# The four context pieces ahead of the first expert product are spread over the first four expert passes

## The chip, the cores and the metric

The kernel runs on one core of a Trainium2 chip. The metric is the device time of one execution in microseconds (us); the time of a kernel is the median of its timed runs. The trace of the kernel before is one further execution, taken with the hardware profiler on. PE is TensorE (PEld its weight loads), DVE is VectorE, ACT is ScalarE, POOL is GpSimd, SP is SyncE; a name with q behind it is the sequencer of that engine.

## What is computed

Two transformer blocks over 256 tokens of width 1024, with 256 context tokens beside them. The first block ends in a mixture of 32 experts, of which each token uses two. The second block begins with a chunkwise mLSTM and a multiscale pool, run for the tokens (x) and for the context. The part of the reference that matters here:

```python
for gi in range(N_GROUPS):
    hid = (jax.nn.silu(jnp.einsum('td,edf->tef', t, w_gate[gi]))
           * jnp.einsum('td,edf->tef', t, w_up[gi])
           * combine[:, gi, :, None].astype(t.dtype))
    out = out + jnp.einsum('tef,efd->td', hid, w_down[gi])
...
ux, uc = hx @ w_in, hc @ w_in
...
hc_f, st_f = mlstm_chunkwise(qc, kc, vc, lif_c, lff_c, zero)
```

The context's side of the second block (uc, its mLSTM, its pool and its output) doesn't depend on the experts, so the kernel computes it while the experts' weights arrive.

## The kernel before

The expert stage (moe_pe, moe_act, moe_dve) runs ten passes over the 32 experts: six passes of four experts each, with 32 columns for every expert, then four passes of two experts (PASSES). Weights are read in halves of 1024 KB. One pass of four experts reads 24 of them: gate, up and down matrices, two halves each, for four experts. A pass has six half products on PE, numbered 6p to 6p+5 in the whole stage: four in project (line L2409: gate half 0, gate half 1, up half 0, up half 1) and two in down (L2426). Every half product raises the semaphore step_used when it is done.

sparse_sync on SP issues the loads of the halves in the order in which PE needs them, into a ring of nine slots (NHALF, half_slot). Load n waits on step_used until the half product that used load n-9 is done (L2282). So nine loads go out at once, and every further group of four waits for a half product of four experts. The context's weights come in halves of the same size through the queue of ACT (f_load, L1402), into four slots of their own. f_next issues the next two halves when ACT takes the last result of the tile that used the slots.

The gather of a pass (L2395) picks the tokens' rows into the pass's 128 columns; ACT copies one half of the result from PSUM to SBUF (L2456), DVE the other (take_gathered). Then come project, SiLU on ACT (L2465), the product with the up half on DVE, four transposes (L2442), ACT's copy of them (L2473), down, and the copies of its result, which ACT stores.

Between these steps each engine runs pieces of the context's work. body_pe, body_act and body_dve are generators, and one next() is one piece. fill(body, p, i) runs the pieces of position i in pass p. PE has nine positions: 0, 1 and 2 behind the first three half products, 3 behind the gather of the next pass, 4 behind the transposes, 5 and 6 behind the halves of down, 7 and 8 at the end of the pass. ACT and DVE have the same nine positions in their own order, so that piece k on one engine answers to piece k on the others. start(body) runs four pieces ahead of the first pass. In all there are 108 pieces in start and fill: 4, 16 for each of six passes, and 2 for each of four.

The context's pieces come in this order on PE: four pieces of the K projection (L1440), four of V (L1455), the gate columns (L1482, L1488), which wait for ACT's exponentials (L1629), then the heads' mLSTM steps (L1499, L1506, L1511 begin a head; L1522, L1527, L1533 follow) with the pieces of the output gate (L1471) in between, and so on to the pool (L1558) and the output projection (L1569, L1574).

Of the kernel before, what the change touches and what calls it, by code (L numbers as in the profile page):

```python
# [227 lines left out]
def build(nc, d, out):  # L228
    ctx = ExitStack()
    with ctx:  # L230
# [601 lines left out]
        def gla_pe(pe):  # L832
# [7 lines left out]
            def tiles(n):  # L840

                for _ in range(n):
                    next(fill)
# [1387 lines left out]
        PASSES = [(N_WIDE + 4 * i, 4) for i in range((NX - N_WIDE) // 4)] + [(2 * i, 2) for i in range(N_WIDE // 2)]  # L2231
# [52 lines left out]
        step_of = [n for n in range(6 * NPASS) for _ in range(PASSES[n // 6][1])]  # L2284

        FILL_FOUR, FILL_TWO = (2, 2, 2, 2, 2, 2, 2, 1, 1), (0, 0, 0, 1, 0, 1, 0, 0, 0)

        def fill(body, p, i):

            for _ in range((FILL_FOUR if PASSES[p][1] == 4 else FILL_TWO)[i]):  # L2290
                next(body, None)

        def start(body):

            for _ in range(4):
                next(body, None)

        def finish(body):
            for _ in body:
                pass  # L2300
# [19 lines left out]
        def moe_pe(pe):  # L2320
            v = pe.value_load(over[0:1, 0:1], min_val=0, max_val=1)
            at = counts()
            with pe.If(v == 0):
                sparse_pe(pe, body_pe(pe))
            after = counts()
            set_back(at)
            with pe.Else():
                dense_pe(pe)
                pe.wait_ge(acc_out, 4 * NX)
                finish(body_pe(pe))  # L2330
            assert counts() == after

        def moe_act(act, chain):
            v = act.value_load(over[0:1, 0:1], min_val=0, max_val=1)
            at, n = counts(), chain.n
            with act.If(v == 0):
                sparse_act(act, body_act(act, chain))
            after, n_after = counts(), chain.n
            set_back(at)
            chain.n = n  # L2340
            with act.Else():
                dense_act(act)
                finish(body_act(act, chain))
            assert counts() == after and chain.n == n_after
# [42 lines left out]
        def sparse_pe(pe, body):  # L2387
            def gather(p):

                pe.wait_ge(pick_ready, p + 1)  # L2390
                if p >= 2:
                    pe.wait_ge(py_out, 2 * p - 2)
                for k in range(DT):
                    for t in range(TT):
                        mm = nc.tensor.matmul(bank[2 + k // 4][:, (k % 4) * P:(k % 4 + 1) * P], hrows[:, t, k * P:(k + 1) * P], pick[:, t, :],  # L2395
                                              start=(t == 0), stop=(t == 1), skip_group_check=True)
                    if k % 4 == 3:
                        mm.then_inc(gath_mm, 1)

            def project(p, b, n, at):  # L2400

                experts = PASSES[p][1]
                w = P // experts
                for half in range(2):
                    pe.wait_ge(step_in[(n + half) % NSTEP], filled_to[n + half])
                    for k in range(4 * half, 4 * half + 4):
                        for e in range(experts):
                            rows = slice(e * w, (e + 1) * w)
                            mm = nc.tensor.matmul(bank[b][rows, :], gath[:, k, rows], half_slot[(load_at[n + half] + e) % NHALF][:, (k % 4) * 512:(k % 4 + 1) * 512],  # L2409
                                                  start=(k == 0), stop=(k == DT - 1), skip_group_check=True)  # L2410
                    mm.then_inc(step_used, 1)
                    if at + half < 3:
                        fill(body, p, at + half)

            def down(p, n):

                experts = PASSES[p][1]
                w = P // experts
                for half in range(2):
                    pe.wait_ge(step_in[(n + half) % NSTEP], filled_to[n + half])  # L2420
                    for f in range(2 * half, 2 * half + 2):
                        for side in range(2):
                            for e in range(experts):
                                rows = slice(e * w, (e + 1) * w)
                                at = (f % 2) * D + side * 512
                                mm = nc.tensor.matmul(bank[2 + side][rows, :], phid_t[:, f, rows], half_slot[(load_at[n + half] + e) % NHALF][:, at:at + 512],  # L2426
                                                      start=(f == 0), stop=(f == 3), skip_group_check=True)
                    mm.then_inc(step_used, 1)
                    fill(body, p, 5 + half)

            gather(0)
            start(body)
            for p in range(NPASS):
                pe.wait_ge(gath_out, 2 * p + 2)
                project(p, 0, 6 * p, 0)
                project(p, 1, 6 * p + 2, 2)
                if p < NPASS - 1:
                    gather(p + 1)
                fill(body, p, 3)
                pe.wait_ge(hid_out, p + 1)  # L2440
                for f in range(4):
                    mm = nc.tensor.transpose(bank[0][:, f * P:(f + 1) * P], phid[:, f * P:(f + 1) * P], ident[:])  # L2442
                mm.then_inc(phid_mm, 1)
                fill(body, p, 4)
                if p < NPASS - 1:
                    pe.wait_ge(gath_out, 2 * p + 4)
                pe.wait_ge(phid_t_out, p + 1)
                down(p, 6 * p + 4)
                fill(body, p, 7)
                fill(body, p, 8)  # L2450
            finish(body)

        def sparse_act(act, body):
            def take_gathered(p):
                act.wait_ge(gath_mm, 2 * p + 1)
                nc.scalar.copy(gath[:, 0:4, :].rearrange("p k s -> p (k s)"), bank[2][:]).then_inc(gath_out, 1)  # L2456

            take_gathered(0)
            start(body)
            for p in range(NPASS):  # L2460
                fill(body, p, 0)
                act.wait_ge(step_used, 6 * p + 2)
                if p:
                    act.wait_ge(phid_mm, p)
                nc.scalar.activation(phid, bank[0][:], ACT.Silu).then_inc(silu_out, 1)  # L2465
                fill(body, p, 1)
                fill(body, p, 2)
                if p < NPASS - 1:
                    act.wait_ge(step_used, 6 * p + 4)
                    take_gathered(p + 1)  # L2470
                fill(body, p, 3)
                act.wait_ge(phid_mm, p + 1)
                nc.scalar.copy(phid_t.rearrange("p f s -> p (f s)"), bank[0][:]).then_inc(phid_t_out, 1)  # L2473
                fill(body, p, 4)
                fill(body, p, 5)
                act.wait_ge(step_used, 6 * p + 6)
                if p:
                    act.wait_ge(rows_stored, 16 * p)
                nc.scalar.copy(py[:, 0:512], bank[2][:]).then_inc(py_out, 1)
                fill(body, p, 6)  # L2480
                act.wait_ge(py_out, 2 * p + 2)
                act.dma_start(expert_rows[p * P:(p + 1) * P, :], py).then_inc(rows_stored, 16)
                for i in (7, 8):
                    fill(body, p, i)
            finish(body)
            act.wait_ge(rows_in, 16 * 4)
            for t in range(TT):
                nc.scalar.activation(acc[:, t, :], acc[:, t, :], ACT.Copy, scale=row_w[:, 0, t:t + 1]).then_inc(rows_scaled, 1)

        def sparse_dve(dve, body, chain):  # L2490
# [10 lines left out]
            def make_pick(p):  # L2501
                o, shape, first, experts, w = slots(p, pick)
                nc.vector.tensor_tensor(o, bc(slot_no[:, 0:w].unsqueeze(1).unsqueeze(1), shape), bc(place[:, :, first:first + experts].unsqueeze(3), shape),  # L2503
                                        ALU.is_equal).then_inc(pick_ready, 1)

            make_pick(0)
            take_gathered(0)
            make_pick(1)
            start(body)
            for p in range(NPASS):  # L2510
                for i in (0, 1, 2):
                    fill(body, p, i)
# [802 lines left out]
```

## Time and profile before

| | us |
|---|---|
| median of 3 timed runs | 1648.13 |
| lowest, highest | 1647.65, 1653.49 |
| the profiled execution | 1652.92 |
| its span | 1650.8 |
| PE busy in the span | 1523.1 |
| DVE busy | 487.8 |
| ACT busy | 341.3 |

The profiled execution took 1652.92 us, of which the span from the first to the last instruction is 1650.8. The expert stage lies between about 476 and 1083 us. A busy PE is a PE that has matmuls in its pipeline, at full or at half clock. In the views of the trace a group's time runs from its first start to its last end, so groups that follow one another overlap by some tenths of a microsecond. The chain of waits counts them without that overlap.

### The profile page before, as it was taken

Reading aid. Unit: us, or ns where it says so; the run is one execution under the profiler, and the core shown is the slowest. Engines: PE = TensorE matmul, PEld = TensorE weight load, DVE = VectorE, ACT = ScalarE, POOL = GpSimd, SP = SyncE. Lnnn points to the kernel's source line nnn. Section 1 sums busy time; section 2 is a strip of 40 time slices with the busy share of each in tenths; the row PEclk is TensorE's granted clock in tenths of the full one; section 3 lists DMA queues with packets and bytes.
Section 4 is the critical chain, followed back from the end, with each engine's and each line's share of the span. In section 5 each row is a group of like instructions: output and inputs, shape, how many; then the busy total and the mean of one; then the engine's idle time right before and its main releaser. Section 6 shows DMA issues by size and latency. Waiting matters only on the chain.

```text
span 1650.8 us, 22126 instructions
## 1 busy us (share of the span) xinstructions
PE 1523.1 (92%) x9357; PEld 1057.2 (64%) x9357; DVE 487.8 (30%) x1233; ACT 341.3 (21%) x698; POOL 4.1 (0%) x8
## 2 busy tenths in 40 slices
PE   6999999999899889988989999969889999999897
PEld 3655689888774444545556655457766675888665
DVE  2200086423343321223213000047342231022571
ACT  2311151211212202022100000023211222021461
POOL 0000000000000000000000000000000000000000
PEclk9999999999799999999999999979899999999998
DMA  9989632132269999999999999932122413423100
GB/s 376 414 348 369 251 137 94 54 108 101 105 281 395 420 420 396 388 420 411 421 413 414 396 400 421 383 135 102 52 102 102 153 71 133 153 84 132 52 1 26
DMA packets 54305, 397.60 MB, mean 241 GB/s; under 512 B 6359, under 2 KB 13688, under 8 KB 16440
## 3 DMA queue, kind: packets, MB, share of 16 engines
q1 hardware_dynamic: 40384, 341.85, 51.4%
q10 hardware_dynamic: 13240, 52.16, 8.0%
q0 software_dynamic: 576, 2.10, 0.4%
q8 instruction: 77, 1.26, 0.3%
q14 instruction: 28, 0.23, 0.0%
HBM read 389.80 MB, written 6.29 MB: 240 GB/s over the span
## 4 chain that ended last, share of the span: by engine, by line
PE 81%; DMA 8%; DVE 4%; ACT 4%; issue 2%; ACTq 1%; SPq 0%; DVEq 0%; POOL 0%; POOLq 0%; PEldq 0%; PEld 0%
PE bank L692 16%; PE bank L1440 13%; PE bank L1455 8%; PE bank L2409 8%; PE bank L2426 4%; PE bank L1574 3%; PE bank L1569 3%; PE bank L526 3%; PE bank L2395 2%; PE bank L723 2%; PE bank L1146 2%; PE bank L1160 2%; DMA ring<-in_moe_w_up 2%; DMA work<-in_pool_inv 1%; PE bank L554 1%
## 5 line engine op out<-in xcount | busy, mean ns | idle before, releaser
L692 PE MATMUL bank<-H,ring 128*128 128x256 f32 (+1 forms) x960 | 245.1, 412 | 1.0 <-ACTq L297 0.7
L692 PEld LDWEIGHTS bank<-H,ring 128*128 128x128 f32 x960 | 181.3, 191 | 52.8 <-issue 28.8
L2409 PE MATMUL bank<-ring,work 128*32 128x512 f32 (+1 forms) x712 | 150.1, 646 | 9.2 <-DMA ring<-in_moe_w_up 5.2
L1440 PE MATMUL bank<-H,work 128*128 128x256 f32 x512 | 115.8, 385 | 1.1 <-issue 1.1
L1440 PE MATMUL bank<-H,ring 128*128 128x256 f32 x512 | 113.6, 381 | 0.0
L2409 PE MATMUL bank<-work 128*32 128x512 f32 (+1 forms) x312 | 109.6, 625 | 1.6 <-DMA work<-in_moe_w_up 1.6
L1440 PEld LDWEIGHTS bank<-H,work 128*128 128x128 f32 x512 | 97.2, 192 | 20.2 <-issue 7.2
L1440 PEld LDWEIGHTS bank<-H,ring 128*128 128x128 f32 x512 | 98.0, 192 | 13.7
L2409 PEld LDWEIGHTS bank<-ring,work 128*32 128x32 f32 (+1 forms) x712 | 40.2, 125 | 85.0 <-issue 72.3
L1455 PE MATMUL bank<-ring,H 128*128 128x512 f32 x192 | 83.4, 593 | 0.0
L2426 PE MATMUL bank<-ring,work 128*32 128x512 f32 (+1 forms) x312 | 69.1, 596 | 0.7 <-issue 0.7
L2426 PE MATMUL bank<-work 128*32 128x512 f32 (+1 forms) x200 | 65.3, 596 | 2.8 <-issue 1.4
L1455 PEld LDWEIGHTS bank<-ring,H 128*128 128x128 f32 x192 | 36.3, 190 | 43.8 <-issue 43.5
L1455 PE MATMUL bank<-work,H 128*128 128x512 f32 x128 | 56.9, 597 | 0.0
L526 PEld LDWEIGHTS bank<-work,csil 128*32 128x32 f32 x1536 | 42.8, 115 | 12.3 <-issue 11.0
L526 PE MATMUL bank<-work,csil 128*32 128x128 f32 x1536 | 49.9, 285 | 0.0
L2395 PEld LDWEIGHTS bank<-work 128*128 128x128 f32 x320 | 38.1, 199 | 11.2 <-issue 7.7
L1455 PEld LDWEIGHTS bank<-work,H 128*128 128x128 f32 x128 | 23.7, 190 | 31.9 <-issue 31.8
L2395 PE MATMUL bank<-work 128*128 128x128 f32 x320 | 40.0, 285 | 3.0 <-DVE work L2503 3.0
L2409 PEld LDWEIGHTS bank<-work 128*32 128x32 f32 (+1 forms) x312 | 26.8, 121 | 24.0 <-issue 22.0
L1522 PE MATMUL bank<-work 128*128 128x257 f32 x64 | 22.5, 436 | 19.7 <-DVE work L1849 16.5
L546 DVE TENSOR_TENSOR mod<-bank,vecs 128x8 f32<-128x8 f32 x24 | 4.0, 167 | 106.7 <-PE bank L537 106.7
(431 smaller groups left out, 2005.0 us busy)
## 6 DMA issues: line engine op xcount, KB each, us to landing
ring<-in_moe_w_gate SPq DMA_DIRECT2D x46, 1024.0 KB, 12.7
ring<-in_moe_w_up SPq DMA_DIRECT2D x43, 1024.0 KB, 11.4
ring<-in_moe_w_down SPq DMA_DIRECT2D x39, 1024.0 KB, 13.0
work<-in_ab_w_in ACTq DMA_DIRECT2D x28, 1024.0 KB, 9.8
ring<-in_ab_w_in SPq DMA_DIRECT2D x14, 2048.0 KB, 7.5
work<-in_moe_w_down SPq DMA_DIRECT2D x25, 1024.0 KB, 14.3
work<-in_ada_w SPq DMA_DIRECT2D x12, 2048.0 KB, 15.5
ring<-in_w_in SPq DMA_DIRECT2D x12, 2048.0 KB, 10.3
```

What stands on the lines that cost most here:

```text
L526: mm = nc.tensor.matmul(bank[5][32 * g:32 * g + 32, 0:P], csil[:, m // 12, k, :], slot_k(mod_chunk[m], k, g * P, (g + 1) * P), start=(k == ...
L692: mm = nc.tensor.matmul(tile_bank(i)[:, 0:n], weight(c, k, j * P, (j + 1) * P), rhs(k), start=(k == 0), stop=(k == kt - 1))
L723: mm = nc.tensor.matmul(bank[i % NB][:], H[:, k, t * P:(t + 1) * P], slot_k(c, k, 0, 512), start=(k == 0), stop=(k == DT - 1))
L1146: mm = nc.tensor.matmul(bank[4 + j % 2][:, half * T:(half + 1) * T], slot_w(c, k, j * P, (j + 1) * P), y[:, k, :], start=(k == 0), stop=(k ...
L1160: mm = nc.tensor.matmul(bank[6 + j % 2][:, 0:T], slot_k(c, k, (j % 4) * P, (j % 4 + 1) * P), mix[:, k, :], start=(k == 0), stop=(k == DT - 1))
L1440: mm = nc.tensor.matmul(b[:, j * T:(j + 1) * T], w_k(m, n, k, at, at + P), H[:, k, m.s], start=(k == 0), stop=(k == DT - 1), skip_group_ch ...
L1455: mm = nc.tensor.matmul(b[:], H[:, k, at:at + P], w_k(m, n, k, 0, 512), start=(k == 0), stop=(k == DT - 1))
L1569: nc.tensor.matmul(b[:, j * T:(j + 1) * T], w_q(m, OUT[r], 8 + k, j * P, (j + 1) * P), m.yp[:, k, :], start=(j + k == 0), stop=False, skip ...
L1574: mm = nc.tensor.matmul(b[:, j * T:(j + 1) * T], w_q(m, OUT[r], k, j * P, (j + 1) * P), m.ym[:, k, :], start=False, stop=(k == 7), skip_gr ...
L2395: mm = nc.tensor.matmul(bank[2 + k // 4][:, (k % 4) * P:(k % 4 + 1) * P], hrows[:, t, k * P:(k + 1) * P], pick[:, t, :], start=(t == 0), s ...
L2409: mm = nc.tensor.matmul(bank[b][rows, :], gath[:, k, rows], half_slot[(load_at[n + half] + e) % NHALF][:, (k % 4) * 512:(k % 4 + 1) * 512] ...
L2426: mm = nc.tensor.matmul(bank[2 + side][rows, :], phid_t[:, f, rows], half_slot[(load_at[n + half] + e) % NHALF][:, at:at + 512], start=(f ...
```

## The change

start is taken out, on all three engines, and with it the four pieces ahead of the first pass. FILL, a list with one row of positions for every pass, takes the place of the choice between FILL_FOUR and FILL_TWO. Its first four rows have 2 instead of 1 at position 7, so that passes 0 to 3 have 17 pieces, not 16. The sum is 108 as before. From pass 4 on, each position holds the same pieces as before.

```diff
         FILL_FOUR, FILL_TWO = (2, 2, 2, 2, 2, 2, 2, 1, 1), (0, 0, 0, 1, 0, 1, 0, 0, 0)
+        FILL = [FILL_FOUR if experts == 4 else FILL_TWO for _, experts in PASSES]
+        FILL[0] = (2, 2, 2, 2, 2, 2, 2, 2, 1)
+        FILL[1] = (2, 2, 2, 2, 2, 2, 2, 2, 1)
+        FILL[2] = (2, 2, 2, 2, 2, 2, 2, 2, 1)
+        FILL[3] = (2, 2, 2, 2, 2, 2, 2, 2, 1)
 
         def fill(body, p, i):
 
-            for _ in range((FILL_FOUR if PASSES[p][1] == 4 else FILL_TWO)[i]):
-                next(body, None)
-
-        def start(body):
-
-            for _ in range(4):
+            for _ in range(FILL[p][i]):
                 next(body, None)
...
             gather(0)
-            start(body)
             for p in range(NPASS):
...
             take_gathered(0)
-            start(body)
             for p in range(NPASS):
...
             make_pick(1)
-            start(body)
             for p in range(NPASS):
```

What this makes of PE's program is shown at two places. The first is the beginning of the expert stage, before (L2395 is the gather, L1440 are K's four pieces, L2409 the first half product):

```order
L2323 COMPARE_AND_BRANCH
L2395 MATMUL bank<-work 128x128 x16
L1440 MATMUL bank<-H,work 128x256 x32
L2409 MATMUL bank<-ring,work 32x512 x2
L2409 MATMUL bank<-work 32x512
```

and now, where "..." stands for the rest of the first half product:

```order
L2323 COMPARE_AND_BRANCH
L2395 MATMUL bank<-work 128x128 x16
L2409 MATMUL bank<-ring,work 32x512 x2
L2409 MATMUL bank<-work 32x512
...
L1440 MATMUL bank<-H,work 128x256 x16
```

Two of K's four pieces now stand behind the first half product and two behind the second.

The second place is PE in pass 0, around its last half product of project (L2409, 16 matmuls), before. Here L1482 and L1488 are the gate columns, L1499 to L1511 begin the first head, L2395 is the gather for pass 1 and L2442 the transposes:

```order
L1482 MATMUL bank<-ident,work 128x64 x8
L1488 MATMUL bank<-work,ident 128x2 x8
L1499 MATMUL bank<-work,ident 128x256 x2
L1506 MATMUL bank<-work 128x128 x4
L1511 MATMUL bank<-ident,work 128x128 x4
L2409 MATMUL bank<-ring,work 32x512 x16
L2395 MATMUL bank<-work 128x128 x16
L1522 MATMUL bank<-work 128x257
L1533 MATMUL bank<-work 128x257 x2
L2442 MATMUL bank<-ident,work 128x128 x4
```

and now (the transposes are on line 2441 there, and L1455 are two pieces of V):

```order
L1455 MATMUL bank<-work,H 128x512 x8
L2409 MATMUL bank<-ring,work 32x512 x16
L2395 MATMUL bank<-work 128x128 x16
L1455 MATMUL bank<-work,H 128x512 x8
L2441 MATMUL bank<-ident,work 128x128 x4
L1482 MATMUL bank<-ident,work 128x64 x8
L1488 MATMUL bank<-work,ident 128x2 x8
L1499 MATMUL bank<-work,ident 128x256 x2
L1506 MATMUL bank<-work 128x128 x4
L1511 MATMUL bank<-ident,work 128x128 x4
```

The gate columns and the first head's beginning moved from ahead of that half product to behind the gather and the transposes, right behind V's last pieces.

## Rows read from the trace of the kernel before

**Rows 1.** The page, busy time of PE and its share.

```profile
PE 1523.1 (92%) x9357; PEld 1057.2 (64%) x9357; DVE 487.8 (30%) x1233; ACT 341.3 (21%) x698; POOL 4.1 (0%) x8
```

**Rows 2.** Windows: length, busy us of each engine, granted clock, DMA share, GB/s.

```profile
461.00:463.00 2.00, 2.00 (x11) 1.65 (x11) 0.34 (x1) 0.00 (x0) 0.00 (x0) 0.95 0.41 66
463.00:466.00 3.00, 3.00 (x15) 2.36 (x13) 0.07 (x1) 0.00 (x0) 0.00 (x0) 1.00 0.93 371
466.00:489.00 23.00, 19.95 (x105) 17.91 (x105) 7.13 (x19) 3.97 (x6) 0.00 (x0) 0.93 1.02 425
489.00:492.00 3.00, 3.00 (x15) 2.66 (x14) 2.75 (x8) 0.59 (x1) 0.00 (x0) 1.00 0.46 186
492.00:496.00 4.00, 4.00 (x19) 3.23 (x18) 3.58 (x14) 0.00 (x0) 0.00 (x0) 1.00 0.00 0
496.00:498.00 2.00, 2.00 (x21) 0.68 (x24) 1.86 (x5) 0.59 (x1) 0.00 (x0) 1.00 0.47 90
499.00:600.00 101.00, 91.53 (x551) 47.10 (x544) 27.12 (x83) 21.07 (x39) 0.00 (x0) 0.93 1.01 420
690.00:698.00 8.00, 8.00 (x43) 2.87 (x43) 0.00 (x0) 0.58 (x1) 0.00 (x0) 1.00 0.68 251
```

**Rows 3.** Timeline of SP: start, length, engine, line, loads issued (start of the first).

```profile
461.28 0.89 SPq L2282 DMA_DIRECT2D ring<-in_moe_w_gate  x2
...
466.09 0.38 SPq L2282 DMA_DIRECT2D work<-in_moe_w_up  x1
499.70 0.81 SPq L2282 DMA_DIRECT2D ring<-in_moe_w_up  x2
```

**Rows 4.** The chain of waits, 476 to 600: start, length, what.

```profile
482.25 13.82 PE bank L1440 x64
496.07 3.57 PE bank L2409 x32
499.64 7.06 PE bank L1455 x16
...
518.24 0.59 ACT work L1614
...
521.31 0.72 PE bank L1482 x8
...
526.26 3.61 PE bank L2409 x32
...
547.50 3.69 PE bank L2426 x32
...
568.62 6.26 PE bank L2409 x32
...
588.53 6.49 PE bank L2409 x32
595.02 3.77 PE bank L2395 x32
```

**Rows 5.** PE's waits, 476 to 1083: releaser, us in total, times, longest.

```profile
PE bank L2409 <- DMA ring<-in_moe_w_up: 5.2, 2, 3.7
PE bank L2409 <- DMA ring<-in_moe_w_gate: 3.9, 2, 2.6
...
PE bank L2409 <- DMA work<-in_moe_w_up: 1.6, 1, 1.6
...
PE bank L2426 <- DMA ring<-in_moe_w_down: 0.7, 1, 0.7
...
PE bank L1482 <- ACT work L1630: 0.4, 1, 0.4
```

**Rows 6.** Timeline of PE in pass 1: start, length, tile, shape, idle before.

```profile
566.58 0.77 PE L1522 MATMUL bank<-work 128*128 128x257 f32 x2 [2.06 <-DVE work L1849]
...
575.73 3.62 PE L1471 MATMUL bank<-work,H 128*128 128x256 f32 x16
...
582.85 0.70 PE L1522 MATMUL bank<-work 128*128 128x257 f32 x2
583.38 1.44 PE L1533 MATMUL bank<-work 128*128 128x257 f32 x4
```

## The prediction, made before the changed kernel ran

> **What bounds the kernel now.** I read the page first: the array's engine, PE, is busy for 1523.1 of 1650.8 us [rows 1], so the end of the kernel moves by what PE has to do or by how long it waits. The change moves no work outside the expert stage and takes none away, so a gain can only be waiting that goes, and a loss waiting that comes. I then read three views of the expert stage, in this order.
>
> The windows [rows 2] show how the weights arrive. A half-weight (an expert's gate, up or down matrix, or a context matrix, comes in halves of 1024 KB, 1.049 MB) takes 1.049/0.42 = 2.5 us of the sixteen DMA engines at 420 GB/s. From 461 to 492 us, 0.13 + 1.11 + 9.78 + 0.56 = 11.6 MB arrive: the nine expert halves that the ring holds and two context halves. Then nothing moves from 492 to 496. The stream is dry from 489 + 0.56/0.42 = 490.3 until about 498 - 0.18/0.42 = 497.6, which is 7.3 us, and from 499 to 600 it never pauses (share 1.01). The cause is in the queue of SP [rows 3]: it issues its ninth load at 466.09 and the tenth at 499.70, because the tenth needs the first product's halves to be used up. The chain of waits [rows 4] shows what PE did meanwhile: the gather ends at 482.25, four context pieces (projections of K) take 13.82 us, and the first half product runs from 496.07 to 499.64.
>
> What that dryness costs is in the list of PE's waits [rows 5]: on expert weights 5.2 + 3.9 + 1.6 + 0.7 = 11.4 us over the whole stage, in six places. Three lie in passes 0 and 1 [rows 4]: at 547.50 (0.7 us), 568.62 (1.3) and 588.53 (3.7). Behind the latter two the half product takes 6.26 and 6.49 us instead of 3.57, since PE ran on its half clock there: 5.6 us more. The other three come later: 1.6 us and 5.2 - 3.7 = 1.5 us in pass 3, 2.6 us in pass 4.
>
> **The change, part by part.** PE's work is the same: 108 pieces before and after. What follows is the same program laid out again with the rows' durations: a half product 3.57 us, a gather 3.77, two pieces of K 13.82/2 = 6.91, two pieces of V 7.06 [rows 4].
>
> *Start.* The gather ends at 482.25 as before, but now the first product needs its copy from PSUM at once. VectorE did not have to hurry before; its copy of that size takes about as long as ScalarE's 0.59 us for 128x512 [rows 4], so I put down 0.85 us of waiting with the hand-over. The half product 0 runs 483.1 to 486.7. The tenth load is then issued at 486.8 rather than 499.70, before the stream is dry: 7.3 us of dryness go.
>
> *Pass 0.* K's pieces to 493.6; half 1 to 497.2; K to 504.1; half 2 to 507.7; V to 514.8; half 3 to 518.4; gather to 522.2; V to 529.3, transposes to 529.7. No weight is late in this stretch: half 1 needs the eighth load, which is among the 11.6 MB that were in by 492, and halves 2 and 3 need loads that follow at 2.5 us each, the sixteenth (with the two context halves that come between) by 490.3 + 9 x 2.5 + a little = 514, before 514.8.
>
> *A new wait.* The gate columns need three exponentials of ScalarE. Before, a half product lay in between and PE waited 0.4 us [rows 5]. Now ScalarE first has to copy the transposed hidden rows and then load a table: from the start of its copy at 518.24 to PE's start at 521.31 that chain took 3.07 us [rows 4]. So PE waits until 532.8, 3.1 us instead of 0.4: 2.7 us more. The gate and mask matmuls take 526.26 - 521.31 = 4.95 us, to 537.8, and half 4 to 541.4.
>
> *A new dryness.* The ring now stands full until half 4 is done. The twenty halves that can be under way by then (sixteen expert, four context) last to 490.3 + 50 = 540.3 by the plain rate; by the landing of before they last to 542.7: the load that PE met at 547.50 was the 24th, the 25th follows 2.5 us later, at 550.0, and 7.3 comes off. The 26th is issued at 541.5 and flows 1.4 us later (the first load of all was issued at 461.28 and had moved 0.13 MB by 463, so it flowed from 462.7), at 542.9. The stream stands still for 0.2 to 2.6 us. Of 7.3 us of lead **5.9 us** are left (4.7 to 7.1).
>
> *What the lead is worth.* At half product 9 PE waits for data before, until 588.53. It will again: with the data wait of 3.70 us, the waits of 0.67, 2.06 and 1.27 and the slow half product (2.7) of passes 0 and 1 gone [rows 4 to 6], and 0.85 + 2.7 us of new waits added, PE would be ready at 588.5 - 3.7 - 6.7 + 3.6 = 581.7 with all its work done. But it has done three pieces fewer (23 against 26): one output gate piece L1471 of 3.55 us and the last two small ones, from 582.85 to 584.82 [rows 6], 5.5 us in all. So it stands there at 576.2, and the weights come at 588.5 - 5.9 = 582.6. It waits some 6 us, here or at the half product ahead of it, and starts 5.9 us earlier with 5.5 us more to do. **The gain at this point is 0.4 us** (from a loss of 0.8 to a gain of 1.6). That is the step the forecast hangs on: the three pieces that filled the waits before are now behind them. The waits that go or come ahead of this point don't count, since the weights set it.
>
> *After it.* Pass 2 has no wait for weights, and from 690 to 698 the DMA share is 0.68 [rows 2]: the stream stands because the ring is full. The lead of the DMA ends there in any case; only PE's 0.4 us goes on. In pass 3 the program is still one piece behind, in passes 4 to 9 it is the same row for row. The three late waits (1.6, 1.5, 2.6) could go altogether (5.7 us, and some 1.4 of slow clock behind the last, half of the 2.7 behind the 3.3 us of waiting at 568.62) or grow by the piece that is owed, 3.5 us. Between a gain of 7.1 and a loss of 3.5 I take 0, since the order of PE and SP around them is nearly the same. The pool weights' wait in pass 5 keeps its distance to its issue.
>
> The sum: 0.4 us less. The profiled execution took 1652.92 us (span 1650.8), which is 4.8 above the median of the three timed runs, 1648.13. Against its own time the sum gives 1652.5, and on the median **1647.7 us**.
>
> A rule of the Trainium skill speaks against the change. After a wait of 2.06 + 1.27 us the trace shows a half product of 6.26 us instead of 3.57 [rows 4, 6]. The Trainium skill, page "TensorE: Matmul & The Clock Gate", section "Loop structure matters more than you think", says that long waits between matmuls leave the array cold, so that what follows runs slowly. By that the gate columns' new wait would make what follows it slow too; without the rule the sum is 1647.7, with it 1650.4, as the first rival works it out from rows.
>
> **The rivals.** *The new wait halves the clock.* It is 3.1 us long, like the 3.3 us ahead of the half product of 6.26 us. If the 4.95 us behind it cost 2.7 more, half 4 ends at 544.1, the stream stands 2.7 us longer, the lead at half product 9 is 3.2 and PE is 2.3 us behind: 1648.13 + 2.3 = 1650.4. Against it: part of that work is tiny matmuls (eight in 0.72 us at 521.31) [rows 4], whose pace a slower clock may not change.
>
> *The late waits go.* PE reaches the end of pass 2 with less context work done, so the ring is refilled earlier where the stream stood still at 690, and its lead covers the waits in passes 3 and 4: 0.4 + 7.1 = 7.5 us, 1640.6. Against it: where PE arrives earlier it also needs the weights earlier.
>
> *Slower: pass 3 starves.* PE comes to the half product of the second late wait with a piece of 3.5 us still to do. If the stream leads by less than 3.5 us there, the wait grows from 1.5 to up to 5 us, the clock falls behind it as at 588.53 (2.9 us more), and the piece is paid later: 3.5 + 2.9 - 0.4 = 6.0 us slower, 1654.1. It decides when the lead is under 3.5 us.
>
> *The dryness stays.* If the tenth load is not issued before 490, or its effect is lost, PE meets half product 9 at the old time with 5.5 us still owed: 1653.6. For it speaks only that SP works in order with 33.6 us between two issues; the order of SP is the same.
>
> **How the numbers follow.** Forecast 0.42, half clock 0.20, late waits go 0.15, pass 3 starves 0.13, dryness stays 0.10. The forecast alone reaches from 1645 to 1650. The range that holds 8 in 10 goes from 1640 to 1655: it takes in the ends of the late waits (1648.13 - 7.5 and + 6.0). A measurement of this kernel can tell some 0.5% (8.2 us) from no change; no case's middle lies beyond that. Half of the late-waits case and a little of the others may overshoot it: faster 0.09, slower 0.09, same 0.82.
>
> **What would show it.** The timeline of SP: the tenth load near 487, the DMA share near 1 from 463 to 540, a short dip near 542. PE: first half product at 483, a wait near 3 us ahead of the gate columns, half product 9 starting near 582.6 behind a wait for weights. It is wrong if half product 9 starts without a wait, or if the waits for weights sum to less than 6 or more than 16 us.

## The result, and the profile after

| | before | after |
|---|---|---|
| median of the timed runs, us | 1651.01 (20 runs) | 1657.89 (20 runs) |
| lowest, highest | 1646.64, 1661.78 | 1652.86, 1671.12 |
| the profiled execution | 1652.92 | 1655.15 |
| its span | 1650.8 | 1653.0 |

The ratio is 1.0048, with a 95% interval of 1.0030 to 1.0066: the changed kernel is 7 to 8 us slower. The profiled execution of after, at 1655.15, is one of its quicker ones, and that of before, at 1652.92, lies above the median, so the traces show only 2.2 us of the loss in their spans. What hides a part of the rest in the traces is told below. Where it goes in a timed run, which leaves no trace, is not shown.

The line of the page that answers to [rows 1] shows the same work on every engine, with PE busy 1.3 us longer:

```profile
PE 1524.4 (92%) x9357; PEld 1060.3 (64%) x9357; DVE 487.5 (29%) x1233; ACT 341.5 (21%) x698; POOL 4.1 (0%) x8
```

The windows of after, with the columns of [rows 2]: length, busy time of PE, PEld, DVE, ACT and POOL, the granted clock, the DMA share, GB/s.

```profile
466.00:489.00 23.00, 19.16 (x111) 14.82 (x110) 7.76 (x20) 3.38 (x5) 0.00 (x0) 0.93 1.01 421
489.00:499.00 10.00, 10.00 (x62) 6.34 (x62) 9.13 (x27) 2.47 (x3) 0.00 (x0) 1.00 1.01 419
499.00:540.00 41.00, 36.98 (x186) 21.83 (x185) 9.40 (x33) 5.24 (x10) 0.00 (x0) 0.90 1.00 414
540.00:548.00 8.00, 7.86 (x56) 3.80 (x59) 2.17 (x8) 2.85 (x8) 0.00 (x0) 0.88 0.18 40
548.00:600.00 52.00, 44.79 (x282) 24.34 (x275) 12.66 (x35) 11.34 (x19) 0.00 (x0) 0.93 1.01 417
```

The dryness of 7.3 us at 490 is gone: the share is 1.01 from 489 to 499. It is back at 540, where a share of 0.18 over 8 us leaves 6.6 us without data. The timeline of SP says why, against [rows 3]: the tenth load goes out at 485.82, 13.9 us sooner than before (0.9 of that because this execution's gather starts sooner), and the 26th at 545.82, 24 us after the 25th (521.52).

```profile
485.82 1.02 SPq L2282 DMA_DIRECT2D ring<-in_moe_w_up  x2
...
521.52 0.33 SPq L2282 DMA_DIRECT2D ring<-in_moe_w_gate  x1
545.82 0.85 SPq L2282 DMA_DIRECT2D work<-in_moe_w_gate  x2
```

The chain of waits, for [rows 4]: start, length, what.

```profile
529.27 0.59 ACT work L1614
529.86 0.49 ACT work L2471
530.37 1.28 ACT L1629
...
532.84 1.12 PE bank L1482 x8
533.95 3.31 PE bank L1488 x16
...
542.03 3.57 PE bank L2426 x32
...
588.91 5.34 PE bank L2409 x32
594.25 3.77 PE bank L2395 x32
```

The list of PE's waits from 476 to 1083, for [rows 5]: releaser, us in total, times, longest.

```profile
PE bank L2409 <- DMA ring<-in_moe_w_up: 6.0, 2, 3.3
...
PE bank L2409 <- DMA work<-in_moe_w_up: 5.1, 2, 2.7
PE bank L1482 <- ACT work L1630: 4.0, 1, 4.0
...
PE bank L2409 <- DMA ring<-in_moe_w_gate: 0.8, 1, 0.8
PE bank L2409 <- DVE work L2491: 0.8, 1, 0.8
```

Waits for expert weights are 11.9 us in all, against 11.4 before, and the wait for the exponentials has grown from 0.4 to 4.0 us. What stands behind that wait is in the timeline of PE (start, length, tile, shape, idle before):

```profile
532.84 1.12 PE L1482 MATMUL bank<-ident,work 64*128 64x64 f32 x8 [4.02 <-ACT work L1630]
533.75 3.52 PE L1488 MATMUL bank<-work,ident 64*128 64x2 f32 x16
537.13 2.05 PE L1499 MATMUL bank<-work,ident 64*128 64x256 f32 x4
539.11 2.07 PE L1506 MATMUL bank<-work 128*128 128x128 f32 x8
540.97 1.06 PE L1511 MATMUL bank<-ident,work 128*128 128x128 f32 x4
```

and the granted clock of that stretch in a window of its own:

```profile
532.80:542.00 9.20, 9.16 (x44) 8.00 (x46) 1.86 (x7) 1.28 (x4) 0.00 (x0) 0.50 0.74 304
```

The clock is 0.50, the lower of its two levels (1.2 GHz), after 4.0 us in which PE stood still. The same matmuls took 4.95 us before [rows 4]; here they take 9.1 (532.84 to 541.97).

### The profile page after: what moved, and what is told of

The parts are those of the page before. It is cut to its first block, busy times and chain, and to the rows that moved or that the text cites. A ratio compares the mean times of both kernels' runs of the same rounds, so it can differ in the third digit from the quotient of the medians.

```text
span 1653.0 us, 22126 instructions
## 1 busy us (share of the span) xinstructions
PE 1524.4 (92%) x9357; PEld 1060.3 (64%) x9357; DVE 487.5 (29%) x1233; ACT 341.5 (21%) x698; POOL 4.1 (0%) x8
## 4 chain that ended last, share of the span: by engine, by line
PE 83%; DMA 6%; DVE 4%; ACT 4%; issue 2%; ACTq 1%; SPq 0%; DVEq 0%; POOL 0%; POOLq 0%; PEldq 0%; PEld 0%
PE bank L692 16%; PE bank L1440 13%; PE bank L1455 8%; PE bank L2409 8%; PE bank L2426 4%; PE bank L1574 3%; PE bank L1569 3%; PE bank L526 3%; PE bank L2395 2%; PE bank L723 2%; PE bank L1146 2%; PE bank L1160 2%; DMA ring<-in_moe_w_up 2%; PE bank L1471 1%; DMA work<-in_pool_inv 1%
## 5 line engine op out<-in xcount | busy, mean ns | idle before, releaser
L2409 PE MATMUL bank<-ring,work 128*32 128x512 f32 (+1 forms) x712 | 148.7, 631 | 12.7 <-DMA ring<-in_moe_w_up 6.0
L1440 PE MATMUL bank<-H,work 128*128 128x256 f32 x512 | 116.1, 385 | 1.4 <-issue 1.4
L1440 PE MATMUL bank<-H,ring 128*128 128x256 f32 x512 | 113.5, 381 | 0.0
L1440 PEld LDWEIGHTS bank<-H,work 128*128 128x128 f32 x512 | 97.0, 192 | 21.3 <-issue 8.4
L2409 PE MATMUL bank<-work 128*32 128x512 f32 (+1 forms) x312 | 108.3, 639 | 0.0
L1440 PEld LDWEIGHTS bank<-H,ring 128*128 128x128 f32 x512 | 98.0, 192 | 13.7
L2409 PEld LDWEIGHTS bank<-ring,work 128*32 128x32 f32 (+1 forms) x712 | 40.2, 122 | 85.8 <-issue 70.4
L1455 PE MATMUL bank<-ring,H 128*128 128x512 f32 x192 | 83.4, 593 | 0.0
L1455 PEld LDWEIGHTS bank<-ring,H 128*128 128x128 f32 x192 | 36.3, 190 | 43.8 <-issue 43.5
L1455 PE MATMUL bank<-work,H 128*128 128x512 f32 x128 | 56.9, 597 | 0.0
L2395 PEld LDWEIGHTS bank<-work 128*128 128x128 f32 x320 | 38.1, 199 | 10.9 <-issue 7.5
L1455 PEld LDWEIGHTS bank<-work,H 128*128 128x128 f32 x128 | 23.7, 190 | 32.1 <-issue 32.0
L2395 PE MATMUL bank<-work 128*128 128x128 f32 x320 | 40.0, 285 | 3.1 <-DVE work L2501 3.1
L2409 PEld LDWEIGHTS bank<-work 128*32 128x32 f32 (+1 forms) x312 | 26.7, 123 | 23.4 <-issue 23.1
## 6 DMA issues: line engine op xcount, KB each, us to landing
work<-in_ab_w_in ACTq DMA_DIRECT2D x28, 1024.0 KB, 10.3
```

Source lines behind the costliest of these rows:

```text
L1440: mm = nc.tensor.matmul(b[:, j * T:(j + 1) * T], w_k(m, n, k, at, at + P), H[:, k, m.s], start=(k == 0), stop=(k == DT - 1), skip_group_ch ...
L1455: mm = nc.tensor.matmul(b[:], H[:, k, at:at + P], w_k(m, n, k, 0, 512), start=(k == 0), stop=(k == DT - 1))
```

## The experiments

All medians are in us, all ratios against the kernel before. I go by the ratios, since a median of 12 runs scatters more (e2's median is above e1's, its ratio below). A ratio of 12 runs has an interval of 3 to 4 us either way, so the difference of two ratios is known to some 5 us. To follow the kernels I give the start of a half product, counted from the start of the first gather (L2395), as difference to before. "Owed" is context work in passes 0 to 3 that before had already done at that point: 5.5 us at half product 9, nothing from half product 24 on. Half product 30 is the first of pass 5, and 35 its last. After has 20 timed runs, e8 has 7, the others 12.

| kernel | ratio | median | hp 4 | hp 9 | hp 24 | hp 30 | hp 35 |
|---|---|---|---|---|---|---|---|
| after | 1.0048 | 1657.89 | +2.5 | +1.3 | +7.6 | +7.9 | +3.4 |
| e1 busy wait | 1.0025 | 1655.32 | -1.5 | -2.7 | +4.3 | +4.9 | +0.7 |
| e2 gate columns behind down | 1.0012 | 1656.87 | -9.0 | -5.8 | +0.7 | -0.8 | -1.2 |
| e10 owed pieces in pass 1 | 0.9997 | 1650.63 | -0.1 | +1.0 | -2.8 | -2.8 | -2.5 |
| e11 both e10 and e1 | 0.9973 | 1647.92 | -1.5 | -0.4 | -3.5 | -2.0 | -5.9 |
| e8 both e10 and e2 | 0.9946 | 1643.20 | -9.0 | -4.3 | -7.4 | -7.4 | -7.4 |

The positions come from one execution of each kernel, and they scatter too. Up to half product 8 after and e10 are the same program, and yet e10 stands 2.7 us ahead at half product 4; e12, the same kernel as e8, stands at -5.3 at half product 30 where e8 stands at -7.4. Behind the expert stage, where no edit reaches, the traces must not be compared at all. From the end of the last half product to the end of the span before and after take 581 us, e1 590 and e2 589. PE's clock is lower there (windows of before, then e2):

```profile
1240.00:1640.00 400.00, 382.92 (x2046) 293.81 (x2044) 118.06 (x337) 111.42 (x266) 0.00 (x0) 1.00 0.24 91
```

```profile
1240.00:1640.00 400.00, 385.30 (x1993) 295.22 (x1992) 118.50 (x337) 109.18 (x261) 0.00 (x0) 0.97 0.24 91
```

The timed runs of e2 lie in two groups of about that distance, five from 1645.5 to 1651.3 and seven from 1656.0 to 1660.1. So how many of 12 runs fell into the upper group is part of the noise in a ratio, and the ratios of e1 and e2 alone would carry little.

**The clock alone.** e1 keeps PE busy through the wait, with matmuls whose result is not used:

```diff
+                if p == 0:
+                    for _ in range(5):
+                        nc.tensor.matmul(bank[1][:], ident[:], hrows[:, 0, 0:512], start=True, stop=True)
```

> The changed kernel, and PE runs five matmuls more (128x512, their result is overwritten unread, 4.4 us) between the transposes of pass 0 and the gate columns, where it waits 4.0 us for ACT. Theory (the wait halves PE's clock, and the slow work holds up the half product that frees ring slots): the gate columns and the first head's beginning take about 5 us instead of 9.1, half product 4 starts some 3.5 us earlier than in the changed kernel (66.1 us after the gather's start there), half product 9 starts 3 to 4 us earlier, and the time falls by 3 to 5 us. Rival (the work there is slow for another reason, its waits for DVE or the order behind V): it stays at 9 us, and the time is the changed kernel's or a little above.

Measured: ratio 1.0025 [0.9999, 1.0051]. The timeline of PE, with the surplus matmuls on L2445:

```profile
530.48 4.46 PE L2445 MATMUL bank<-work,ident 128*128 128x512 f32 x10
534.86 0.71 PE L1482 MATMUL bank<-ident,work 64*128 64x64 f32 x8
535.42 1.90 PE L1488 MATMUL bank<-work,ident 64*128 64x2 f32 x16
```

The wait is as long, yet what follows takes 4.9 us again, and half product 4 starts 4.0 us sooner than in after. So the clock fell because PE stood still. By the ratios it is worth 1.0048 - 1.0025 = 0.23%, 3.8 us, about half of the loss. That difference alone is not clear of the noise. What makes it firm is that the 4.0 us are in the trace at half product 4 and still 3.3 at half product 24, and that the same step comes out once more below.

**Wait and clock.** e2 puts the gate columns behind the first half of down, where the exponentials are long done. PE's position 4 of pass 0 is empty and position 5 has four pieces:

```diff
-        FILL[0] = (2, 2, 2, 2, 2, 2, 2, 2, 1)
+        FILL[0] = (2, 2, 2, 2, 0, 4, 2, 2, 1)
```

> The changed kernel with row 0 of FILL as (2, 2, 2, 2, 0, 4, 2, 2, 1): the gate columns' and the first head's pieces stand behind half product 4 instead of ahead of it. Theory (the lead of the weights is lost because half product 4 comes late behind wait and slow clock): half product 4 starts near 54 us after the gather's start instead of 66, the stream has no pause, its lead over the kernel before at half product 9 is 4 to 7 us, and the time is 5 to 7 us under the changed kernel's, equal to the kernel before within 2 us. Rival (the loss comes from the owed pieces alone, or from pass 3 on): the time stays within 2 us of the changed kernel's.

Measured: 1.0012 [0.9986, 1.0037], 5.9 us under after by the ratios, and half product 9 leads by 5.8 us, both as expected. Half product 4 comes 11.5 us sooner than in after, since besides wait and clock (8.2) the pieces themselves (4.9) now stand behind it, less a new wait of 1.6 there for ScalarE's copy. But at half product 9 it still waits 3.7 us for weights, and at 24 it is no better than before: 5.5 us of owed work are in it.

**The owed pieces alone.** e10 is after with the pieces that passes 1 to 3 owe all put behind the third half product of pass 1:

```diff
-        FILL[1] = (2, 2, 2, 2, 2, 2, 2, 2, 1)
-        FILL[2] = (2, 2, 2, 2, 2, 2, 2, 2, 1)
-        FILL[3] = (2, 2, 2, 2, 2, 2, 2, 2, 1)
+        FILL[1] = (2, 2, 5, 2, 2, 2, 2, 1, 1)
```

> The changed kernel, with the three pieces that passes 1 to 3 owed all put behind the third half product of pass 1 (position 2 has 5 pieces, rows 2 and 3 are FILL_FOUR). The wait for the gate columns in pass 0 stays as it is in the changed kernel. Theory (two terms that add: the slow clock behind the gate columns' wait, and the owed pieces): half product 9 waits 2.7 us in the changed kernel and then takes 5.3 instead of 3.6 us; the owed 5.5 us now cover that wait. It starts 5.5 - 2.7 = 2.8 us later and runs 1.8 us faster with nothing owed, so from half product 10 on this kernel is 5.5 - 2.8 + 1.8 = 4.5 us ahead of the changed one: some 1653.5 us, and half product 24 at 7.5 - 4.5 = +3 us against before. Rival (the owed pieces fill later waits anyway, so where they stand is nothing): half product 24 stays at +7.5 and the time at 1658. Rival (the loss is all in the gate columns' wait and the owed pieces cost their full 5.5 + 1.8): half product 24 at 0, time 1651.

Measured: 0.9997 [0.9975, 1.0020], 8.4 us under after where 4.5 were expected. Half product 24 was expected at +3 and stands at -2.8, so the figures of the second rival (half product 24 at 0, 1651 us) fit better. At half product 10 it is 1.5 us ahead of after by the table's measure. Less 2.7 us by which this execution was already ahead at half product 4, and with the 5.9 us that after owes there, that is 4.7: up to here as expected. The rest comes later. After still waits and slows down in pass 3 (its timeline of PE there):

```profile
742.78 2.28 PE L2409 MATMUL bank<-ring,work 128*32 128x512 f32 x9 [3.29 <-DMA ring<-in_moe_w_up]
...
761.40 0.67 PE L1522 MATMUL bank<-work 128*128 128x257 f32 x2 [2.17 <-DVE work L1849]
```

```profile
742.78:748.12 5.34, 5.34 (x33) 1.36 (x33) 0.00 (x0) 0.00 (x0) 0.00 (x0) 0.68 1.01 417
```

That half product takes 5.34 us at a clock of 0.68, and e10's takes 3.6 behind a wait of 1.35:

```profile
738.77 1.49 PE L2407 MATMUL bank<-ring,work 128*32 128x512 f32 x12 [1.35 <-DMA ring<-in_moe_w_up]
```

By half product 24 after is 7.6 us behind e10 (10.3 less the 2.7).

**Both, and both with the clock alone.** e8 has the edits of e2 and e10; e12 is the same kernel timed again on another chip, and e11 has those of e1 and e10.

> The kernel e2_gate_behind_down with the three pieces that PE owes given back ahead of half product 9: row 1 is (2, 2, 5, 2, 2, 2, 2, 1, 1), rows 2 and 3 as before. Theory (three owed pieces of 5.5 us eat the 5.8 us of lead): half product 9 starts 3.5 to 5.5 us before the kernel before's with nothing owed, PE is 3 to 5 us ahead from there to pass 5, and the time is 2 to 5 us under the kernel before. Rival (the pieces, put together, wait for DVE and ACT and lose it again): half product 9 starts within 2 us of the kernel before's, and the time is equal to it or above.

> The kernel with the owed pieces in pass 1, the wait for the gate columns left where it is, and five surplus matmuls of 128x512 behind the transposes of pass 0 that keep PE busy through that wait (their result is not used). It splits what moving the gate columns gave in that schedule (ratio 0.9997 to 0.9946, some 8.4 us) into wait and clock. Theory (half of it is the clock, since the clock doubles 4.95 us of work and delays the 26th load by the same 4.1 us): half product 4 comes 4 us earlier than with the wait left idle, half product 24 some 4 us earlier, and the ratio is near 0.997 (1646 us). Rival (the clock is nothing where nothing is owed, the stream has enough lead): ratio 0.9997, 1650.6 us. Rival (it is all the clock): 0.9946, 1643 us.

> The kernel with the gate columns behind down and the owed pieces in pass 1 once more, on the same chip as the one before it in this list, since it had only 7 timed runs. If the two terms (gate columns' wait with its slow clock, owed pieces) are real, it is again at 1643 us, ratio 0.9946 within 0.002. If its 7 runs were lucky ones, it comes out near the 1648.4 us of the kernel that has only the gate columns moved and the pool's rows laid out.

Measured: e8 0.9946 [0.9923, 0.9968] from 7 runs, e12 0.9972 [0.9949, 0.9995] from 12, with a median of 1645.29. The 19 runs together have a median of 1645.13, and the mean of the two ratios is 0.9959. e12 misses its 0.9946 within 0.002 by a little, so the first figure was on the lucky side, but the kernel beats before in both. e8 gained more than its expected 2 to 5 us. e11: 0.9973 [0.9952, 0.9994], as expected. Its trace shows less of it than was expected: half product 4 comes 1.4 us sooner than e10's and half product 24 0.8, not 4 each, since e10's execution was ahead by 2.7. In e8 the stream never stops, neither at 490 nor at 541 (windows):

```profile
489.00:541.00 52.00, 50.37 (x295) 29.25 (x294) 21.09 (x65) 7.70 (x13) 0.00 (x0) 1.00 1.01 420
541.00:550.00 9.00, 6.77 (x41) 2.69 (x43) 2.71 (x8) 2.72 (x8) 0.00 (x0) 0.81 1.01 420
```

and of the 11.4 us of waits for expert weights 5.3 are left, none of them in passes 0 and 1:

```profile
PE bank L2407 <- DMA ring<-in_moe_w_gate: 2.5, 1, 2.5
...
PE bank L2407 <- DMA ring<-in_moe_w_up: 1.6, 1, 1.6
PE bank L2407 <- DMA work<-in_moe_w_up: 1.2, 1, 1.2
```

Each term but the last now comes out more than once, from ratios times 1651 us (e8 and e12 as their mean):

| term | worth, us |
|---|---|
| slow clock behind the gate columns' wait | after to e1 3.8; e10 to e11 4.0 |
| the wait and the clock | after to e2 5.9; e10 to e8 6.3 |
| the owed pieces | after to e10 8.4; e1 to e11 8.6; e2 to e8 8.8 |
| what is left, the early start | before to e8 6.8 |

That -6.8 + 6.3 + 8.4 = +7.9, after's loss, shows nothing by itself: it is the way from before over e8 and e10 to after, and comes out whatever the terms are. What is a test is the agreement within a row, that an edit is worth the same in two kernels. There are two such tests, after, e1, e10 and e11 (3.8 against 4.0, or 8.4 against 8.6, which is the same test) and after, e2, e10 and e8 (5.9 against 6.3). With some 5 us of uncertainty on each term the agreement is better than they can promise. The last row is what is left when both terms are gone. It is not the early start alone, since e8 has a small new wait of its own (1.6 us, that for ScalarE's copy).

**Other ways to place the pieces.** e3 puts all 20 pieces into pass 0 (rows 1 to 3 are FILL_FOUR):

```diff
-        FILL[0] = (2, 2, 2, 2, 2, 2, 2, 2, 1)
+        FILL[0] = (3, 3, 2, 3, 3, 2, 2, 1, 1)
```

> No pieces ahead of the first product, and all four given back within pass 0: row 0 is (3, 3, 2, 3, 3, 2, 2, 1, 1), the other rows as before, so that from the end of pass 0 on every position holds what it holds in the kernel before. Theory (an early first product is worth its 7 us of DMA if nothing is owed afterwards and the gate columns stay covered by a half product and the gather): half product 9 starts 4 to 7 us earlier than before, and the time is 2 to 6 us under the kernel before. Rival (PE, not the weights, sets the time, so the early start is worth nothing): equal to the kernel before within 1.5 us.

e4 leaves two pieces in front of the first product (on all three engines) and gives one each to passes 0 and 1 (against before):

```diff
-            for _ in range(FILL[p][i]):
+            for _ in range((FILL_FOUR if PASSES[p][1] == 4 else FILL_TWO)[i] + (p < 2 and i == 7)):
                 next(body, None)
+
+        def start(body):
+
+            for _ in range(2):
+                next(body, None)
```

> Half of the change: two pieces stay ahead of the first product, passes 0 and 1 have 17 pieces. Theory (the loss is made by the gate columns' place behind the gather, which needs all four pieces moved): here the gate columns' piece comes two positions later than before and one half product after V's last piece is not between them any more, so a part of the wait comes too; first product near 13.3 us after the gather's start, stream pause cut by 7 us; time between the kernel before and the changed one, 0 to 5 us above the kernel before. Rival (the loss grows with the number of owed pieces alone): half of the changed kernel's loss, 3 to 4 us above.

Measured: e3 1.0058 [1.0039, 1.0077], 9.6 us slower where it was expected to gain 2 to 6; e4 1.0026 [1.0006, 1.0047], 4.3 us slower, which fits both its theory and, within the noise, its rival, so it doesn't tell them apart. In e3 the heads' first steps come so early that PE waits for VectorE, and PE runs at nearly half its clock through all of it (timeline of PE, then the window):

```profile
539.41 1.20 PE L1522 MATMUL bank<-work 128*128 128x257 f32 x2 [1.71 <-issue]
546.87 1.20 PE L1522 MATMUL bank<-work 128*128 128x257 f32 x2 [3.69 <-DVEq L1890]
```

```profile
530.00:553.00 23.00, 17.60 (x66) 14.00 (x67) 8.90 (x36) 4.72 (x10) 0.00 (x0) 0.55 0.52 217
```

So paying everything at once is no cure: the pieces have to stand where their inputs are ready. e4 has half of the early start (half product 0 is 6.9 us earlier instead of 13.0) and still loses, at half product 24 by 2.6 us.

**The pool's wait.** From half product 30 to 35 after gets back 4.5 of its 7.9 us, in the profiled execution. Before, then after, around the pool's first matmuls (timeline of PE):

```profile
863.55 3.75 PE L1558 MATMUL bank<-work 128*128 128x256 f32 x8 [7.12 <-issue]
```

```profile
863.99 1.97 PE L1558 MATMUL bank<-work 128*128 128x256 f32 x8 [0.60 <-issue]
```

Both start at 864. PE waits there for VectorE's first pooled rows, and VectorE waits for a table of 512 KB (in_pool_inv) that ACT loads right behind the pool's weights, 1 MB in rows of 1 KB (timeline of DVE, before, then after):

```profile
859.97 1.30 DVE L1961 TENSOR_TENSOR_SCAN work<-work 128x548 f32<-128x548 f32 x1 [37.67 <-DMA work<-in_pool_inv]
```

```profile
860.41 1.30 DVE L1961 TENSOR_TENSOR_SCAN work<-work 128x548 f32<-128x548 f32 x1 [31.16 <-DMA work<-in_pool_inv]
```

After issues the two loads 7.0 us later (842.28 against 835.32) and has them at nearly the same time, since the weights take 14.4 us to land instead of 23.4 and the table 17.7 instead of 24.2. So PE, which comes 7 us later, waits 6.5 us less. Why the loads were quicker there is not shown; just before them the DMA engines were not full (260 GB/s from 838 to 842, where before moved 416 GB/s in the same stretch ahead of its own, 831 to 835). How a timed run fares at this place is not known: e12's trace has a wait of 6.3 us there where e8's, the same kernel, has 7.4.

e5, e6 and e7 are before, after and e2 with those weights laid out anew, so that each partition reads one run of 8 KB (the loads read them so); e9 is e8 with it:

```diff
-    a["ab_pool_w_2"] = i["ab_pool_w_2"][0]
+    a["ab_pool_w_2"] = i["ab_pool_w_2"][0].reshape(len(POOLS), 2, P, MD).transpose(2, 0, 1, 3).reshape(P, 2 * len(POOLS), MD)
```

> The kernel before, with the pool's weights laid out in memory so that each partition reads one run of 8 KB instead of eight of 1 KB. Theory (the pool's wait of 7.1 us in pass 5 comes from the small packets of that load beside the expert loads): the pool's weights land within 12 us of their issue instead of 23, the wait of 7.1 us is gone, the half product after it starts 6 to 9 us earlier, and the time is 5 to 8 us under the kernel before. Rival (expert weights are late next): under 3 us.

> The changed kernel with the same layout of the pool's weights. Theory (the change loses 7.9 us by pass 5, of which the profiled run got 4.5 back at the pool's wait): without that wait to absorb it, the loss against e5_before_pool_rows is the full 6 to 8 us, and the time is 0 to 3 us under the changed kernel's. Rival (the loss is made behind the pool): the two stand 3 us apart or less.

> The kernel e2_gate_behind_down with the same layout of the pool's weights. Theory: equal to e5_before_pool_rows within 2 us (e2 stood 0.8 us ahead of the kernel before at the pool), so 4 to 8 us under the kernel before. Rival (e2's order itself costs 2 us): 2 us above e5_before_pool_rows.

> The kernel with the gate columns behind down and the owed pieces in pass 1, and beside it the pool's second weights laid out so that each partition reads one run of 8 KB. Theory (the pool's load crawls because of its 1 KB rows, and its wait of 7.4 us is paid in that kernel in full, with a slow clock behind it): the load lands in about 9 us, the wait goes, and the kernel ends 5 us earlier, less the 2 to 6 us that the up weights are then waited for, as in the kernel before with the same layout (1647.2 against 1651.0): some 1639.5 us, ratio 0.992. Rival (where nothing is owed, the weights set the time behind pass 5 and the pool's wait only hides that): the same 1643.2.

Measured: e5 0.9973 [0.9957, 0.9990], e6 1.0016 [0.9995, 1.0037], e7 0.9976 [0.9955, 0.9997], e9 0.9946 [0.9920, 0.9971] with a median of 1641.58. e6 against e5 is 0.43%, 7.1 us, so after's loss is about the same with the pool's wait away, as expected, and the timed runs of after against before show no sign of what the pool's wait gave back in the trace. e5 gains 4.5 us, less than the expected 5 to 8, e6 lies 5.3 us under after where 0 to 3 were expected, e7 equals e5 as expected, and e9 misses its 0.992 and equals its rival's figure. The rows of the DMA view from 830 to 865 (KB each, median us to landing), before, then e5, and after from 825 to 866:

```profile
work<-in_ab_pool_w ACTq DMA_DIRECT2D x1, 1024.0 KB, 23.4
```

```profile
work<-in_ab_pool_w ACTq DMA_DIRECT2D x1, 1024.0 KB, 9.2
```

```profile
work<-in_ab_pool_w ACTq DMA_DIRECT2D x1, 1024.0 KB, 14.4
```

The wait goes, but e5 then waits for expert weights a little later (timeline of PE), and e9 does so for 5.93 us:

```profile
870.10 1.06 PE L2409 MATMUL bank<-work 128*32 128x512 f32 x1 [6.12 <-DMA ring<-in_moe_w_up]
```

So the pool's wait hides a shortage of weights, and part of what it costs comes back behind it (from e5's lead over before of 10.7 us at half product 31 4.8 are left at 35). e9's median is the lowest of all, but its interval and that of e8 and e12 overlap: whether the layout gains anything there stays open.

## Why the prediction was wrong, step by step

*Forecast 1647.7 us in a range to 1655; measured 1657.89.* Of the 10.2 us between the two, 2.9 are the base: the forecast counted from the median of three runs of before, 1648.13, and over twenty it is 1651.01. That part says nothing of the mechanism. The rest is the change itself: after lost 7.9 us by the ratio where a gain of 0.4 was forecast, and the top of the range stood 6.9 above the forecast's own base. The forecast's sum was that gain of 0.4 us from 5.9 of lead and 5.5 of owed work. The runs put what the early start leaves at 6.8, the gate columns at 6.3 (of which 1.4 was in the lead of 5.9), and the owed work at 8.4.

*Right: the start.* The tenth load was foreseen at 486.8 and went out at 485.82; the wait for the gathered copy was foreseen as 0.85 and was 0.8; no weight was late in pass 0. The 7.3 us of dryness at 490 did go, and e8 shows what that is worth when nothing else is in the way.

*Wrong: the 4.95 us of the gate and mask matmuls.* This is the step that failed first: the sum took the work behind the new wait at full clock. It took 9.1, at a clock of 0.50. The wait ahead of them was 4.0 us, not 3.1, since ScalarE had a second copy ahead of the exponentials (L2471, 0.49 us) that the chain taken from before lacked, and began the first one 0.46 us after PE had stopped (528.81 to 529.27): 3.07 + 0.49 + 0.46 = 4.0. The rival "the new wait halves the clock" had the mechanism and a chance of 0.20, but it put the slow clock at 2.7 us, taken from a half product that was partly slow, and set tiny matmuls aside; these slowed too (L1488 from 1.9 to 3.5 us, L1482 from 0.7 to 1.1). The Trainium skill, page "TensorE: Matmul & The Clock Gate", section "Loop structure matters more than you think", says that what follows a long wait between matmuls runs slowly; e1 agrees with it, where the same wait filled with work left the clock at full speed.

*Wrong, by the same step: the lead.* With the 26th load issued at 545.82, not 541.5, and the last data in at about 540, the stream stood still for 6.6 us, where 0.2 to 2.6 were foreseen. So the dryness moved, and of 7.3 us of lead almost nothing was left: half product 9 started 1.3 us later than before (from the gather), where 5.9 earlier was forecast. The bound of 4.7 to 7.1 for the lead did not include the rival's price, and should have.

*Half right: the owed pieces.* The 5.5 us at half product 9 were read rightly from the trace of before. What was missed is their price behind that point. Taking the change of the late waits in passes 3 and 4 as 0 was wrong: the rival "pass 3 starves" happened in part, with a wait of 3.3 us and a half product of 5.34. The owed work cost 8.4 us in the timed runs, not 5.5. It costs next to nothing where PE would wait anyway: at half product 10 e8, which has done it, stands at -7.2 in the trace, and e2, which still owes it, at -7.4.

*Wrong in the trace alone: the pool's wait.* It did not keep its distance to its issue: from the issue of the pool's weights to PE's start it is 28.2 us before and 21.7 after. The wait shrank from 7.1 to 0.6 us, and of the 7.9 us by which the profiled execution stood behind, 3.4 were left at half product 35. The ratio of the timed runs is 7.9 us all the same; why they don't show this is open.

*The other rivals.* The dryness did not stay for want of an early issue: it went at 490 and came back at 541. The late waits did not go in after; in e8 5.3 us of them are left.

## What to carry to other kernels

A transfer that starts earlier is only worth what the next full ring leaves of it: follow the stream to the next place where it stops, and price that place with the engine's slow clock in it. Work that filled a wait is not free to move; put it back where the next wait stands, which here took away the loss of 7.9 us, and with the gate columns moved as well left a gain of about 7. And before a trace is believed on a few microseconds, take a second one of the same kernel: here two executions of the same program differed by 2 to 3 us at one place, and the same work behind the stage took from 578 to 590 us. And when an idle engine's wait can't be avoided, look at what is queued behind it: 4 us of standing still cost another 4 in what followed.

## What the runs showed of the hardware

- After 4.0 us without a matmul PE's clock was granted at 0.50 for the next 9.2 us, though PE was busy for 9.16 of them. The small matmuls slowed like the large ones, or nearly so: eight of 64x64 took 1.12 us instead of 0.71, sixteen of 64x2 3.52 instead of 1.90, eight of 128x128 2.07 instead of 1.16. With the gap filled by 128x512 matmuls there was no fall.
- A load of 1 MB in rows of 1 KB took 23.4 us beside the experts' loads (before), 21.0 and 23.6 in two executions of one kernel (e12, e8), and 14.4 in after; as rows of 8 KB it took 9.2 (e5, e6). From 830 to 865 the stream as a whole ran at 412 GB/s before and 421 in e5, so the small rows kept that load waiting far more than they slowed the stream.
- After the ring had stood full, the next load of after landed 5.0 us after its issue at 545.82, and the ones behind it some 2.5 us apart. The bytes came slowly at first: 115, 147, 344 and 418 GB/s in the four microseconds from 546 on.
- Behind the expert stage the same matmuls ran at a mean granted clock of 1.00 in some executions and 0.97 in others (1240 to 1640, before and e2), and the stretch from the last half product to the end took 581 against 589 us. What decides which it will be is not shown.
